# PEER experts: every expert computed on TensorE from the table read in order, in place of gathered rows

## What is computed

```python
N_KEYS, PEER_HEADS, PEER_TOPK = 128, 8, 16       # 128*128 = 16384 experts in each layer
q   = (t @ w_pq).reshape(n, 8, 2, 128)
sub = einsum('nhpd,hpkd->nhpk', q, peer_keys)    # two lists of 128 scores for each head
sc, ix = top_k(sub, 16)
cand    = sc[:, :, 0, :, None] + sc[:, :, 1, None, :]
cand_ix = ix[:, :, 0, :, None] * 128 + ix[:, :, 1, None, :]
best, pos = top_k(cand.reshape(n, 8, 256), 16)
experts = take_along_axis(cand_ix, pos)          # 8*16 = 128 experts for each token
gates   = softmax(best)
act = gelu(einsum('nd,nhkd->nhk', t, peer_u[experts]))
out = einsum('nhk,nhkd->nd', gates * act, peer_v[experts])
```

## Time and profile before

| | us |
|---|---|
| median of 3 runs | 6044.92 (6032.94 to 6048.27) |
| span of the profiled execution (first to last instruction) | 6013.1 |
| `experts`, first layer | 1136.6 to 2993.3 |
| `experts`, second layer | 4133.8 to 5983.8 |
| PE busy over the span | 4653.2 (77%) |
| DVE, ACT, POOL busy | 3331.5, 1398.9, 1716.5 |
| moved by the transfers | 1452 MB, of it 1342 MB by the indirect ones |

### The profile page before, as it was taken

The page is one execution under the profiler, slowest core; times in us unless marked ns, Lnnn a source line. Parts: engine busy times, 40 slices in busy tenths (PEclk is TensorE's granted clock), DMA queues, the critical chain, the costliest instruction groups (busy, mean ns, idle before and its releaser), DMA issues. The chain is left out here.

```text
span 6013.1 us, 55155 instructions
## 1 busy us (share of the span) xinstructions
PE 4653.2 (77%) x15196; PEld 2430.6 (40%) x15196; DVE 3331.5 (55%) x8542; ACT 1398.9 (23%) x3534; POOL 1716.5 (29%) x1570
## 2 busy tenths in 40 slices
PE   8788988877677777777697889888777777777776
PEld 3588654422222222222245875544222222222222
DVE  4555561366565666666455555513656656666564
ACT  1211541222121221222112125412222222122221
POOL 0022000144343443434301220002443434444343
PEclk9888999999898898999898889998998988999898
DMA  6000001499898998999760000014998989989897
GB/s 241 17 3 1 14 29 53 169 380 377 341 368 336 375 374 336 371 355 383 313 229 1 3 14 1 29 63 179 376 373 345 375 344 370 373 356 382 342 381 290
DMA packets 239910, 1452.23 MB, mean 242 GB/s; under 512 B 25120, under 2 KB 30880, under 8 KB 75296
## 3 DMA queue, kind: packets, MB, share of 16 engines
q0 software_dynamic: 184320, 1342.26, 57.2%
q1 hardware_dynamic: 55456, 108.20, 5.2%
HBM read 1446.80 MB, written 3.57 MB: 241 GB/s over the span
## 5 line engine op out<-in xcount | busy, mean ns | idle before, releaser
L1483 PE MATMUL psall<-region,diag 128*128 128x512 f32 x5120 | 2630.2, 668 | 1019.1 <-ACT diag L1462 1005.4
L1427 DVE CUSTOM_DVE_ANT_0 region<-region,hcur 128x1024 f32<-128x1024 f32 x1280 | 1567.4, 1225 | 1220.0 <-DMA region<-in_peer_uv,stage 1183.8
L1483 PEld LDWEIGHTS psall<-region,diag 128*128 128x128 f32 x5120 | 1044.6, 212 | 2604.7 <-ACT diag L1462 1410.3
L1392 POOL DMA_INDIRECT region<-in_peer_uv,stage x1280 | 1479.5, 1156 | 1725.0 <-PE psall L1483 1429.6
L1454 ACT ACTIVATE act<-dot 128x2 f32<-128x2 f32 x640 | 130.2, 203 | 2647.1 <-DVE dot L1427 2647.1
L1462 ACT ACTIVATE diag<-cons,wgt 128x128 f32<-128x128 f32 x1280 | 435.0, 393 | 244.7 <-DVE wgt L1438 230.7
L1386 POOL COPY stage<-eidx 128x8 uint32 x160 | 60.5, 378 | 1475.6 <-PE psall L1472 1076.0
L450 POOL TENSOR_TENSOR mlt<-lt,cons 128x512 f32<-128x512 f32 x120 | 174.4, 1463 | 474.4 <-DVE lt L536 336.3
L1324 PE MATMUL psall<-region 128*128 128x512 f32 (+1 forms) x1024 | 281.3, 438 | 29.5 <-DMA region<-in_w_pq 29.5
L1324 PEld LDWEIGHTS psall<-region 128*128 128x128 f32 x1024 | 157.2, 195 | 149.9 <-issue 119.6
L337 PE MATMUL psall<-wring,hT 128*128 128x512 f32 (+1 forms) x480 | 202.7, 581 | 5.7 <-DVE hT L262 5.7
(11 more groups left out here) (295 smaller groups left out, 4980.4 us busy)
## 6 DMA issues: line engine op xcount, KB each, us to landing
mixed<-in_w_mod SPq DMA_DIRECT2D x32, 1024.0 KB, 5.3
region<-in_peer_uv,stage POOLq DMA_INDIRECT x1280
wring<-in_w_mod SPq DMA_DIRECT2D x8, 2048.0 KB, 12.3
region<-in_w_pq SPq DMA_DIRECT2D x8, 2048.0 KB, 11.8
wring<-in_w_in_tm SPq DMA_DIRECT2D x4, 2048.0 KB, 13.0
region<-in_w_out SPq DMA_DIRECT2D x4, 2048.0 KB, 11.3
wring<-in_w_in_fm SPq DMA_DIRECT2D x2, 2048.0 KB, 8.3
wring<-in_w_in_tm SPq DMA_DIRECT2D x2, 1728.0 KB, 9.4
```

Source lines behind the costliest of these rows:

```text
L1392: nc.gpsimd.indirect_dma_start(out=p.uv[:, s, :], out_offset=None, in_=d["peer_uv"], in_offset=bass.IndirectOffsetOnAxis(ap=p.stage[:, hal ...
L1427: nc.vector.tensor_tensor_reduce(out=p.uv[:, s % H, 0:D], in0=p.uv[:, s % H, 0:D], in1=p.hcur[:, :], scale=1.0, scalar=0.0, op0=ALU.mult, ...
L1483: mm = nc.tensor.matmul(ps[c], p.diag[:, s % H, :], p.uv[:, s % H, D + 512 * c:D + 512 * c + 512], start=False, stop=False, skip_group_che ...
```

## The change

`experts` is replaced by two blocks, and the picking moves.

- **Picking.** `top_pairs` does for one tile and head what `route_piece` did (the copy of the scores to `r_sub` is gone; the rest stays, as one chain). `route` does it for two heads of every tile, ten in all; the other thirty follow in the next block. What is kept for each of a token's 128 slots is i, j and the exponent of the gate (`slots`), not a row number.
- **`dots_and_gates`.** The 16384 rows of `peer_u`, laid out beforehand so that 128 experts with the same i are one block with features on partitions, are read in order, 128 blocks of 512 KB, into a ring of five. For each block PE makes 16 matmuls with weights of 128x128 from the table and 320 moving columns of `h2T` (8 steps of features, two halves of the tokens), ACT applies gelu, and SP stores the 128x640 activations to DRAM (`mid_acts`, 0.33 MB). In between PE builds a dense table of gates: for each token the outer product of two one-hot matrices over its 128 slots (`hot_j` against `hot_i`, the latter times the gate), one 128x128 matmul for a token; DVE makes the one-hots 8 tokens at a time with three operations of 1024 elements, ACT copies the product into `gstage`, and SP stores `gstage` whenever 64 tokens are full (4.19 MB, ten times a layer, `mid_gates`). One such batch of 8 tokens follows every 1.38 blocks from block 17 on. `gstage` is one buffer: the first copy of the next 64 tokens waits for the store.
- **`weigh_rows`.** In 16 chunks of 8 blocks: SP loads the activations (2.62 MB), the gates (2.62 MB, in runs of 2 KB) and the 1024 rows of `peer_v` (two loads of 2.1 MB); DVE multiplies activations with gates (8 operations of 640 elements); PE makes 10 sums of 8 matmuls with 512 moving columns; DVE adds each sum to `ysum`, in the last chunk times `gt2` and onto `x`.
- POOL has no work in PEER any more; the semaphores cleared at a layer's end are 159.

The diff, cut:

```diff
-            with pool.Fori(0, NT) as t:
-                with pool.Fori(0, NH) as h:
-                    head(t, h, t * NH + h)
...
+            for t in range(NT):
+                dve.wait_ge(sem("r_out"), at[("s", 0, t, 0)] + 1)
+                for h in range(HEADS_EARLY):
+                    top_pairs(p, own, t, h)
...
+def dots_and_gates(p, lay):
+    for b in range(BLOCKS):
+        jobs.append(("u", b))
+        if b == FIRST_G - 1:
+            jobs.append(("turn", 0))
+        while n < N_G and b >= FIRST_G + int(1.38 * n):
+            jobs.append(("g", n))
...
+            for j in range(BLOCKS + 2):
+                if j < BLOCKS:
+                    if j >= UROWS:
+                        sp.wait_ge(sem("u_mm"), j - UROWS + 1)
+                    sp.dma_start(p.uring[:, j % UROWS, :, :], d["u_t"][bass.ds(lay, 1), j].rearrange("l p k n -> p (l k) n")
+                                 ).then_inc(sem(f"load_u{j % UROWS}"), 16)
+                b = j - 2
+                if b >= 0:
+                    sp.wait_ge(sem("act_out"), b + 1)
+                    sp.dma_start(d["acts"][b], p.aring[:, b % AROWS, :]).then_inc(sem(f"store_a{b % AROWS}"), 16)
+                    for half in halves_after.get(b, ()):
+                        sp.wait_ge(sem("gate_out"), (half + 1) * (HALF // BATCH))
+                        sp.dma_start(d["gates"][half], p.gstage[:, :, :]).then_inc(sem("store_g"), 16)
...
+                own.link(nc.vector.tensor_tensor(p.hot_i[:, n % 2, :, :], bc(cols[0], 2, P), bc(p.io128, 1, BATCH), ALU.is_equal))
+                nc.vector.tensor_tensor(p.hot_j[:, n % 2, :, :], bc(cols[1], 2, P), bc(p.io128, 1, BATCH), ALU.is_equal)
+                nc.vector.tensor_tensor(p.hot_i[:, n % 2, :, :], p.hot_i[:, n % 2, :, :], bc(cols[2], 2, P), ALU.mult).then_inc(sem("hots"), 1)
...
+                    for half in range(2):
+                        out = p.psall[:, u_bank(i) + 512 * half:u_bank(i) + 512 * half + TOK // 2]
+                        for k in range(KT):
+                            last = nc.tensor.matmul(out, p.uring[:, i % UROWS, k, :], p.h2T[:, k, half * (TOK // 2):(half + 1) * (TOK // 2)],
+                                                    start=(k == 0), stop=(k == KT - 1))
...
+                    for c in range(BATCH):
+                        last = nc.tensor.matmul(p.psall[:, g_bank(i) + c * P:g_bank(i) + (c + 1) * P], p.hot_j[:, i % 2, c, :],
+                                                p.hot_i[:, i % 2, c, :], start=True, stop=True)
...
+def weigh_rows(p, lay):
+                w = p.wact[:, c % 2, b, :].rearrange("p (h t) -> p h t", t=HALF)
+                nc.vector.tensor_tensor(w, w, p.wgate[:, c % 2, :, b, :], ALU.mult).then_inc(sem("weighed"), 1)
...
+            for c in range(CHUNKS):
+                pe.wait_ge(sem("weighed"), GROUP * (c + 1))
+                for half in range(2):
+                    m = 2 * c + half
+                    pe.wait_ge(sem(f"load_vt{m % VRING}"), 16 * (m // VRING + 1))
+                    for t in range(NT):
+                        n = JOBS * c + NT * half + t
+                        if n >= 8:
+                            pe.wait_ge(sem("y_out"), n - 7)
+                        for b in range(GROUP):
+                            last = nc.tensor.matmul(ps[n % 8], p.wact[:, c % 2, b, t * P:(t + 1) * P], p.vring[:, m % VRING, b, :],
+                                                    start=(b == 0), stop=(b == GROUP - 1))
```

More of the change, by code:

```diff
@@ new lines, in dots_and_gates @@
+    N_G = NT * PER_TILE
+    jobs = []
+    n = 0
+    for b in range(BLOCKS):
[4 more added lines that the diff above has]
+            jobs.append(("g", n))
+            if n % PER_TILE == PER_TILE - 3 and n // PER_TILE < NT - 1:
+                jobs.append(("turn", n // PER_TILE + 1))
+            n += 1
+    jobs += [("g", m) for m in range(n, N_G)]
+    halves_after, b = {}, 0
+    for kind, i in jobs:
+        if kind == "u":
+            b = i
+        elif kind == "g" and (i + 1) % (HALF // BATCH) == 0:
+            halves_after.setdefault(b, []).append(i // (HALF // BATCH))
@@ new lines, in u_bank, with g_bank, _ @@
+    def u_bank(b):
+        return 1024 * (b % 2)
+    def g_bank(n):
+        return 2048 + 1024 * (n % 2)
+    with nc.Block() as block:
+        @block.sync
+        def _(sp):
+            for j in range(BLOCKS + 2):
[11 more added lines that the diff above has]
+                        sp.dma_start(d["gates"][half], p.gstage[:, :, :]).then_inc(sem("store_g"), 16)
+            for r in range(AROWS):
+                sp.wait_ge(sem(f"store_a{r}"), 16 * (BLOCKS // AROWS))
+            sp.wait_ge(sem("store_g"), 16 * 2 * NT)
@@ new lines, in _ @@
+            for h in range(HEADS_EARLY, NH):
+                top_pairs(p, own, 0, h)
+            shares(0)
+            for t in range(NT):
+                for q in range(PER_TILE):
+                    one_hots(t * PER_TILE + q)
+                    if t + 1 < NT:
+                        if q % 2 == 0 and q // 2 < NH - HEADS_EARLY:
+                            top_pairs(p, own, t + 1, HEADS_EARLY + q // 2)
+                        if q == 12:
+                            shares(t + 1)
+        @block.tensor
@@ L1464, in _, with gate_out @@
-            with act.Fori(0, NT * NH - AHEAD) as n:
-                head(n, True)
-            with act.Fori(NT * NH - AHEAD, NT * NH) as n:
-                head(n, False)
+            def gate_out(n):
+                act.wait_ge(sem("g_mm"), n + 1)
+                half, c = divmod(n * BATCH, HALF)
+                if c == 0 and half >= 1:
+                    act.wait_ge(sem("store_g"), 16 * half)
+                nc.scalar.activation(p.gstage[:, :, c:c + BATCH],
+                                     p.psall[:, g_bank(n):g_bank(n) + BATCH * P].rearrange("p (t i) -> p i t", t=BATCH),
+                                     ACT.Copy).then_inc(sem("gate_out"), 1)
```

409 lines of the change are left out of this document (203 added, 206 removed).

## The result

The changed kernel takes 7080.59 us (median; 7078.46 to 7083.66) where the kernel before took 6038.93 us in the same comparison (6018.93 to 6048.27): a ratio of 1.1726, 95% interval 1.1699 to 1.1753. It is slower, by 1042 us. The profiled execution took 7082.25 us, its span is 7080.5.

A forecast was written before the change was run, and what follows sets the result against it. Gather transfers bound the kernel before; PE would bound the new one. A layer: 15.8 + 7.3 + 1253.6 + 33.9 + 1099.0 + 2.5 = 2412.1 us; span 7133, plus 31.8 makes 7165 us, range 7125 to 7290.

The forecast's parts named there:

- the last paragraph of the forecast: Signs: L1422 at 270 ns, L1556 at 429, PE busy over 0.95 in both stretches, clock 1.00, transfers near 0.35.
- The two large terms: PE's time in each layer: 1253.6 us for dots_and_gates and 1099.0 us for weigh_rows.
- The interpolated 270.4 ns for 320 columns: PE's pace for the table's matmuls in dots_and_gates, taken between 111.5 ns (128 columns) and 429.3 ns (512).
- the rivals: Stores in the way (0.14), DVE as the bound (0.03), clock not holding (0.03), long streams overlapping (0.02).
- the forecast's sum for it, 18.5 us of 21: SP's queue in dots_and_gates: gates' store and block load there after 18.5 us, needed after about 21; no stall.
- under a fifth: ACT's gelu and copies in dots_and_gates, even at 4 us a copy, stay under a fifth of PE's time.
- the clock held: Rival: clock fails over 1.1 ms without pause; at 0.90 adds 261 us a layer, 7690 us; chance 0.03.
- the step of the earlier trace did not shrink: Rival: long matmul streams overlap, pace below 429 ns for 512 columns; time about 5305 to 5310 us; chance 0.02.
- the median stands 31.8 above the span: Last step of the sum: 31.8 us added to the forecast span of 7133 us, giving 7165 us.
- a head's picking takes ... 10.2: DVE's picking of one head: 10.6 us from first to last operation, less the copy 10.2.
- The term of 15.8 us in a layer: Start of dots_and_gates: ten heads picked in route end at 1152.4, PE free at 1136.6, so PE waits 15.8 us.
- The handover: Between dots_and_gates and weigh_rows: stores 7 us, meeting 1, loads 17.5, multiplications 6.6, clock 1.8; 33.9 us a layer.

The follow-up runs named there:

- The first experiment: The kernel before, unchanged, run again in ten executions, each with its own span: median 6033.93 us, ratio to before 0.9994.

## Why the prediction was right, and where it failed

**Right: the bound and the mechanism.** PE at its own pace, the clock at 1.00, the transfers near 0.35 (0.33 and 0.35), both stretches above 0.95 busy: as the last paragraph of the forecast asked. The two large terms, 1253.6 and 1099.0 us, came from streams of 128 and 512 columns in `route`, and measured 1249.8 and 1101.2 with the lower clock of the first instructions in them. The interpolated 270.4 ns for 320 columns was 269.4.

**Right: the rivals fell.** No block waited for a store (PE waited for `in_u_t` only at the starts), and the forecast's sum for it, 18.5 us of 21, had 16.3 to 17.6 of 20.6; DVE had 526 us of work in 1250; ACT had 188 (the forecast's "under a fifth" did not follow from its 4 us, since 80 copies of 4 us are 320 of 1254, but a copy took 1.0 us); the clock held; and the step of the earlier trace rows did not shrink in a run of 2560, 428.8 ns. So the rule of the Trainium skill, page "TensorE: Matmul & The Clock Gate", section "Back-to-back issue gap", does not hold for this kernel: even rounded operands, one instruction a matmul, give 223.5 ns for 512 columns in a stream, not the roughly 131 of the page but near its 216 for a single gap.

**Wrong: "the median stands 31.8 above the span".** This step cost 30 of the 84 us. The forecast added to a new span what separated one span from the median of other executions. Between an execution and its own span lie 1.8 us, and the profiled one of after shows it too (7082.25 and 7080.5). The text had said that the profile does not give the profiled execution's time, and then took one of the two possible readings without a bound for the other; a range that held both would have begun 30 us lower. (The first experiment showed it.)

**Wrong: "a head's picking takes ... 10.2".** The term of 15.8 us in a layer is 0, which is 31.6 of the 84 us. The forecast took the duration from the same operations in the kernel before, but the change had written their loop out, so that the waits between them are on constants and three of them are gone. This difference in the code was costed at nothing. Measured: 8.48 us with constants, 9.63 with registers, and each microsecond of DVE past PE's end counted in full (83 us for five more heads in each layer). The forecast had looked for its own error elsewhere, in the pace for 320 columns and in stalls; neither was it.

**Mis-sized, all towards dear.** The start had the engines' meeting twice and a first load of 4.5 us: 4.64 us in all between PE's scores and its first block, where 22.2 were forecast, 15.8 of them for picking. `dots_and_gates` was 5.6 us shorter than forecast (4.1 from the 320 columns, 1.7 from the transposes, 0.3 from the gates, the clock 0.5 the other way). The handover took 27.1 us where 32.1 were forecast without the clock: stores and meeting 4.9 instead of 8, since the last store of gates landed in 11.1 us instead of 12.6 and the last activations only 0.8 us behind it instead of some 2; loads 16.2 instead of 17.5; multiplications 6.03 instead of 6.6. The way into the next layer cost 0.45 us more than before, where 1.2 were forecast for the eighteen semaphores. PE's first matmul there, which waits for DVE, before and after:

```profile
3015.35 4.49 PE L295 MATMUL psall<-cons,xn 128*128 128x128 f32 x24 [22.85 <-DVE xn L245]
...
3546.83 6.18 PE L308 MATMUL psall<-cons,xn 128*128 128x128 f32 x32 [24.65 <-DVE xn L258]
```

It starts 3546.83 - 3524.35 = 22.48 us behind the last addition to `x`, before 3015.35 - 2993.32 = 22.03. SP's first load comes 3.5 us later than before (3537.48 - 3524.35 = 13.1 us behind the addition, where it was 9.6), but this matmul does not wait for it.

**The sum of the miss.** 17.5 at the start, 5.6, 4.6 in the handover with `weigh_rows`, and 0.35 at the end are 28.1 us a layer, 56.1 in both; outside the stages the span grew by 6.2 us instead of 2.4, of which 3.8 lie before the first layer's `route` ends (1139.50 against 1135.67; the unchanged kernel of the first experiment took 1141.4). So the span was 52.4 us shorter than forecast; 30 are the term around the span; 1.7 the distance of the profiled execution from the median. Together 84. Without either of the two wrong steps alone the time would still have been outside the range, whose lower end allowed 20 us a layer for PE, loads and starts; without both it would have been inside.

## What to carry to other kernels

Take the profiled execution's span as nearly its time, and build the forecast on that one execution: the distance between one span and a median is scatter until a second execution shows otherwise. Adding the predicted change to the median is no way out where the replaced part itself scatters: here it gives the same 7165 us. When a loop is written out, the waits become others, and fewer, even if the operations stay, so take a chain's duration as a bound and not as a value. Before a gather is replaced by a dense product, see how many instructions a matmul becomes for its type: here this alone decided between 17% slower and 25% faster.

## What the runs showed of the hardware

- A chain of short DVE operations (0.3 to 0.7 us each) costs 0.09 us more for each step that waits against a register which is then raised, than for one that waits on a constant: 9.63 against 8.48 us for thirteen such steps in a head. A wait on a register costs 0.20 us more than none (0.40 against 0.20 us from one start to the next).
- A matmul of 32-bit floats is two instructions, each of 428.8 ns for 512 columns and 269.4 for 320; with operands rounded by the engine that writes them it is one, of 223.5 and 151.9 ns: factors of 3.84 and 3.55. The Trainium skill, page "FP8 and Floating Point Precision", section "TensorE Precision Notes", states four passes through the array for true FP32; these factors come near four.
- PE kept the 2.4 GHz level for 1.1 ms of dense work (granted clock 1.00 in 1101.2 us). Behind a stall of 5.8 to 6.6 us the next block took 1.5 to 3 us longer, a quarter to a half of the stall itself; in the two such blocks that were read, the granted clock was 0.75 and 0.83 on the mean.
- A load of 512 KB landed in 3.6 us at the median and, beside a second stream of the same size, in 4.1; behind one store of 4.2 MB on its queue it took up to 14.2 us, and behind two it made PE wait about 6 us.
